# Output weights split inside the mixer's end, the last gate block after the last scores, and the first two feature tiles fetched early, in a one-core decoder layer

## The reference

```
u = x @ w_in                                # q, k, v | xr (LRU input) | yg (gate branch)
attn = sliding_window_attention(rope(q), rope(k), v, sinks)    # window 128, 8 heads, 2 kv heads
xc = causal_depthwise_conv(xr)                                 # width 4
r, i = sigmoid(xc @ w_rg + b_rg), sigmoid(xc @ w_ig + b_ig)
a = exp(-8 * r * softplus(-lam));  h_t = a_t * h_(t-1) + sqrt(1 - a_t^2) * i_t * xc_t
lru = gelu(yg) * h
mixed = concat(rmsnorm(attn) * g_attn, rmsnorm(lru) * g_lru)
h = layernorm(alpha * x + mixed @ w_out)
scores = sigmoid(h @ w_router)              # 64 experts, 8 of them chosen within 4 of 8 groups
out = layernorm(alpha * h + shared_expert(h) + sum over chosen experts of weight * expert(h))
```

## Time and profile before

| what | value |
|---|---|
| median of 3 runs | 2626.66 us |
| lowest, highest | 2623.69, 2627.61 us |
| the profiled execution | 2624.12 us |
| its span (first to last instruction) | 2622.3 us |
| busy in the span | PE 93%, PEld 75%, DVE 60%, ACT 44%, POOL 27% |
| mean granted TensorE clock | 0.965 of full speed |
| mixer | 0 to 535.8 us |
| `output_and_route` | 535.8 to about 795 us |
| `experts` | the largest part of the rest |

### The profile page before, as it was taken

The page is one execution under the profiler, slowest core; times in us unless marked ns, Lnnn a source line. Parts: engine busy times, 40 slices in busy tenths (PEclk is TensorE's granted clock), DMA queues, the critical chain, the costliest instruction groups (busy, mean ns, idle before and its releaser), DMA issues. The chain is left out here.

```text
span 2622.3 us, 48850 instructions
## 1 busy us (share of the span) xinstructions
PE 2441.9 (93%) x11925; PEld 1975.1 (75%) x11927; DVE 1569.2 (60%) x2501; ACT 1148.2 (44%) x1761; POOL 707.0 (27%) x830
## 2 busy tenths in 40 slices
PE   7899999769987989999999999999999999999990
PEld 5676767648875867888888888888888888888870
DVE  4675756647777865655565555665555555655526
ACT  4636363532212124544555444554555445554425
POOL 0000000001110003333344333343333333433435
PEclk9999999979998999999999999999999999999995
DMA  7232322174426437987888878898888878888656
GB/s 225 92 133 93 121 89 89 47 236 163 162 101 230 165 135 236 280 238 211 253 274 255 241 221 238 254 276 231 256 252 258 240 218 247 271 254 237 140 115 272
DMA packets 261956, 527.82 MB, mean 201 GB/s; under 512 B 26960, under 2 KB 172272, under 8 KB 257792
## 3 DMA queue, kind: packets, MB, share of 16 engines
q1 hardware_dynamic: 211088, 344.67, 38.3%
q0 software_dynamic: 47952, 179.70, 27.2%
q10 hardware_dynamic: 2848, 2.59, 0.4%
HBM read 388.99 MB, written 137.92 MB: 201 GB/s over the span
## 5 line engine op out<-in xcount | busy, mean ns | idle before, releaser
L2109 POOL DMA_INDIRECT acc<-y,si x164 | 298.4, 1820 | 783.6 <-DMA acc<-y,si 387.7
L2198 DVE TENSOR_TENSOR gu_lo<-raw_gu,gu_hi (+1 forms) x128 | 292.8, 2288 | 175.4 <-ACT gu_hi L2129 175.1
L2306 PE MATMUL psG<-gu_hi,xT_lo 128*128 x1320 | 348.3, 406 | 0.9 <-issue 0.8
L2295 PE MATMUL psG<-gu_hi,xT_hi 128*128 x1328 | 338.6, 397 | 3.1 <-ACT xT_hi L2125 1.6
L2295 PE MATMUL psG<-gu_lo,xT_hi 128*128 x1328 | 336.0, 395 | 0.0
L2295 PEld LDWEIGHTS psG<-gu_hi,xT_hi 128*128 128x128 f32 x1328 | 250.5, 189 | 64.1 <-issue 3.7
L2295 PEld LDWEIGHTS psG<-gu_lo,xT_hi 128*128 128x128 f32 x1328 | 249.9, 188 | 60.3
L2306 PEld LDWEIGHTS psG<-gu_hi,xT_lo 128*128 128x128 f32 x1320 | 236.6, 189 | 45.3 <-issue 1.3
L2129 ACT ACTIVATE gu_hi<-raw_gu (+1 forms) x128 | 238.1, 1908 | 47.2 <-issue 47.2
L2198 DVE TENSOR_TENSOR d_lo<-raw_d,d_hi (+1 forms) x64 | 146.7, 2293 | 150.0 <-ACT d_hi L2129 150.0
L2178 ACT ACTIVATE HT_hi<-psH 128x256 fp32r<-128x256 f32 x164 | 63.0, 384 | 381.2 <-PE psH L2313 381.2
(11 more groups left out here) (324 smaller groups left out, 3851.3 us busy)
## 6 DMA issues: line engine op xcount, KB each, us to landing
raw_gu<-in_w_gate_dram SPq DMA_DIRECT2D x64, 1024.0 KB, 6.0
raw_gu<-in_w_up_dram SPq DMA_DIRECT2D x64, 1024.0 KB, 12.2
raw_d<-in_w_down_dram SPq DMA_DIRECT2D x64, 1024.0 KB, 6.5
wring<-split_d SPq DMA_DIRECT2D x24, 1024.0 KB, 4.8
acc<-out SPq DMA_DIRECT2D x17, 512.0 KB, 3.0
split_d<-wring SPq DMA_DIRECT2D x8, 1024.0 KB, 4.9
mT<-mixed SPq DMA_DIRECT2D x16, 512.0 KB, 3.7
xt<-in_x_dram SPq DMA_DIRECT2D x16, 512.0 KB, 4.4
```

Source lines behind the costliest of these rows:

```text
L2109: nc.gpsimd.indirect_dma_start(out=acc, out_offset=bass.IndirectOffsetOnAxis(ap=si[k][:, 0:1], axis=0), in_=y[k][:], in_offset=None, compu ...
L2198: nc.vector.tensor_tensor(dst, src, hi, ALU.subtract).then_inc(dlo_s if n == 2 else gulo_s, 1)
L2295: nc.tensor.matmul(psG[slot][:], xT_hi[slot][:, c, :], right[:, bass.ds(w, 1), c, :].rearrange("p a n -> p (a n)"), start=(n == 0 and c == ...
L2306: m = nc.tensor.matmul(psG[slot][:], xT_lo[slot][:, c, :], gu_hi[:, bass.ds(w, 1), c, :].rearrange("p a n -> p (a n)"), start=False, stop= ...
```

## The change

- `wqkv`, `wring`, `xT`, `IG` and `A` are allocated before the mixer at fixed sides of the memory, and given back at once, so that `raw_gu`, `raw_d`, `wo_hi` and `wo_lo` lie on the same bytes: `wqkv_hi` and `IG` under `raw_gu`, `wring[0]` under the first slot of `raw_d`, `A` and `wqkv_lo` under `wo_hi`, `xT` under `wo_lo`. The buffer `mT` is now in that first slot of `raw_d` for all tiles.
- SP fetches three of the four pieces of `w_out` when the last k and v product is full, features 0 and 1 when gate block 2 is full, and the fourth piece when the last scan is over.
- ACT makes all eight `wo_hi` at the end of the mixer, between the last `lr_square` and `square_o(15)`. DVE makes four `wo_lo` behind `evac_o(15)`, and the other four as the first thing of the next block.
- In the last group, gate block 2 is cut in halves around the last scores, and gate block 3 comes behind them. `gelu(3)` goes behind `exps(15)`, the last `gate` behind `divide(15)`, and `evac_p(15)` ahead of the four `lru_norm`.
- `output_and_route` no longer fetches `w_out` and features 0 and 1; ACT's first copy there is `high(0)`.

```
@@ mixer, sync
+                if g + 1 == GROUPS:
+                    U["kv", TILES - 1].wait_full(sp_)
+                    for q in range(3):
+                        load_wo(q)
                 store_attention(i + 2)
                 if g + 1 < GROUPS:
                     load_split(1, g + 1)
+            U["yg", 2, GROUPS - 1].wait_full(sp_)
+            for n in range(2):
+                sp_.dma_start(mixed_view(raw_d, n), mixed[n]).then_inc(mixed_in[n], 16)
+            sp_.wait_ge(scan_s, LC * GROUPS)
+            load_wo(3)
             store_recurrent(GROUPS - 1)
             store_attention(TILES - 1)
@@ mixer, scalar
             exps(TILES - 1)
+            gelu(3, GROUPS - 1)
             for c in range(LC):
                 lr_square(c, GROUPS - 1)
+            for c in range(KC):
+                act.wait_ge(wo_in[c // 2], 32 if c < 4 else 16)
+                nc.scalar.activation(wo_hi[:, c, :], wo_view(raw_gu)[:, c, :], ACT.Copy).then_inc(wohi_s, 1)
             square_o(TILES - 1)
@@ mixer, vector
-                for c in range(LC):
+                for c in range(LC if g < GROUPS - 1 else LC - 1):
                     gate(c, g)
             divide(TILES - 1)
+            gate(LC - 1, GROUPS - 1)
+            evac_p(TILES - 1)
             for c in range(LC):
                 lru_norm(c, GROUPS - 1)
-            after_turn(TILES - 1)
+            evac_o(TILES - 1)
+            U["yg", LC - 1, GROUPS - 1].wait_full(dve)
+            for c in range(KC // 2):
+                dve.wait_ge(wohi_s, c + 1)
+                nc.vector.tensor_tensor(wo_lo[:, c, :], wo_view(raw_gu)[:, c, :], wo_hi[:, c, :],
+                                        ALU.subtract).then_inc(wolo_s, 1)
             sums(GROUPS - 1)
@@ mixer, tensor
-                tile(i + 3, lambda: project_T(6, g), last_filler)
+                if g < GROUPS - 1:
+                    tile(i + 3, lambda: project_T(6, g), last_filler)
+                else:
+                    tile(i + 3, *halves(6, g))
+                    project_T(7, g)
@@ output_and_route, sync
-            load_wo(0)
-            load_mixed(0)
-            for q in range(1, HALF):
-                load_wo(q)
             load_x(0)
-            load_mixed(1)
             load_x(1)
             sp.wait_ge(wolo_s, KC)
             prefetch(sp)
@@ output_and_route, scalar
-            for c in range(KC):
-                act.wait_ge(wo_in[c // 2], 32 if c < 4 else 16)
-                nc.scalar.activation(wo_hi[:, c, :], wo[:, c, :], ACT.Copy).then_inc(wohi_s, 1)
-                if c == 0:
-                    high(0)
+            high(0)
             scale_x(0)
@@ output_and_route, vector
+            for c in range(HALF, KC):
+                dve.wait_ge(wohi_s, c + 1)
+                nc.vector.tensor_tensor(wo_lo[:, c, :], wo[:, c, :], wo_hi[:, c, :], ALU.subtract).then_inc(wolo_s, 1)
+            low(0)
             dve.wait_ge(consts_set, 5)
             nc.vector.reciprocal(rms[:], rms[:]).then_inc(consts_set, 1)
             dve.wait_ge(consts_set, 6)
-            for c in range(KC):
-                dve.wait_ge(wohi_s, c + 1)
-                nc.vector.tensor_tensor(wo_lo[:, c, :], wo[:, c, :], wo_hi[:, c, :], ALU.subtract).then_inc(wolo_s, 1)
-                if c == 1:
-                    low(0)
             dve.wait_ge(consts_in, 16 * 6)
             low(1)
```

More of the change, by code:

```diff
@@ L91, in bcast, with wo_view, mixed_view @@
     return bass.AP(tensor=ap.tensor, offset=ap.offset, ap=pairs)
+def wo_view(raw_gu):
+    return raw_gu[:].rearrange("p s k n -> p (s k n)").rearrange("p (k n) -> p k n", n=D)
+def mixed_view(raw_d, n):
+    return raw_d[:, 0, n, :].rearrange("p (k n) -> p k n", k=KC)
 def mixer(nc, x, w_in, conv_w, conv_b, w_rg, b_rg, w_ig, b_ig, lam, sinks, g_attn, g_lru,
-          ident_h, cos_h, sin_h, mask_h, maskf_h, split_d, mixed, ssa, ssl):
+          ident_h, cos_h, sin_h, mask_h, maskf_h, split_d, mixed, ssa, ssl,
+          w_out, raw_gu, raw_d, wo_hi, wo_lo, shared, early):
+    wo_in, wohi_s, wolo_s, mixed_in = early
     spent = []
@@ L1130, in output_and_route @@
         consts_set = sem("consts2_set")
-        mixed_in = [sem(f"mixed_in{i}") for i in range(2)]
         xt_in = [sem(f"xt_in{i}") for i in range(2)]
@@ L2556, in decoder_layer, with sbu @@
         passed = ctx.enter_context(nc.semaphore("passed"))
-        spent = mixer(nc, x, w_in, conv_w, conv_b, w_rg, b_rg, w_ig, b_ig, lam, sinks, g_attn, g_lru,
-              ident_h, cos_h, sin_h, mask_h, maskf_h, split_d, mixed, ssa, ssl)
+        with ExitStack() as under:
+            def sbu(name, shape, dt, side):
+                return under.enter_context(nc.sbuf_tensor(name, shape, dt, side=side))
+            wqkv_hi = sbu("wqkv_hi", [P, KC, XR_COL], FR, "left")
+            IG = sbu("IG", [P, LC, GT], F, "left")
+            wring = [sbu(f"wring{i}", [P, 2, KC, P], FR, "left") for i in range(2)]
+            A = sbu("A", [P, LC, GT], F, "right")
+            wqkv_lo = sbu("wqkv_lo", [P, KC, XR_COL], FR, "right")
+            xT = [sbu(f"xT_{n}", [P, KC, GT], FR, "right") for n in ("hi", "lo")]
+        shared = ([wqkv_hi, wqkv_lo], wring, xT, IG, A)
         raw_gu = sb("raw_gu", [P, W_SLOTS, KC, 2 * FE])
         raw_d = sb("raw_d", [P, W_SLOTS, FE // P, D])
+        early = ([ctx.enter_context(nc.semaphore(f"wo_in{i}")) for i in range(KC // 2)],
+                 ctx.enter_context(nc.semaphore("wohi_s")), ctx.enter_context(nc.semaphore("wolo_s")),
+                 [ctx.enter_context(nc.semaphore(f"mixed_in{i}")) for i in range(2)])
+        out_weights = ExitStack()
+        wo_hi, wo_lo = (out_weights.enter_context(nc.sbuf_tensor(n, [P, KC, D], FR, side="right")) for n in ("wo_hi", "wo_lo"))
+        spent = mixer(nc, x, w_in, conv_w, conv_b, w_rg, b_rg, w_ig, b_ig, lam, sinks, g_attn, g_lru,
+              ident_h, cos_h, sin_h, mask_h, maskf_h, split_d, mixed, ssa, ssl,
+              w_out, raw_gu, raw_d, wo_hi, wo_lo, shared, early)
         loaded = [ctx.enter_context(nc.semaphore(n)) for n in ("gate_in", "up_in", "down_in")]
```

69 lines of the change are left out of this document (33 added, 36 removed).

## The result

| | before | after |
|---|---|---|
| median | 2626.02 us (4 runs, 2623.69 to 2627.61) | 2608.56 us (4 runs, 2606.57 to 2609.98) |
| profiled execution, its span | 2624.12, 2622.3 us | 2607.80, 2606.0 us |
| mean granted clock | 0.965 | 0.970 |

The ratio is 0.9934, with a 95% interval of 0.9922 to 0.9946: 17.5 us less. The forecast was 2605 (2600 to 2613), so the time lies in the range, 3.6 us above the forecast.

What follows compares the result with a forecast made beforehand. It took the mixer-to-output-stage seam, where PE is hardly at work and nothing hides a delay, as the bound. Terms -4.15 - 6.95 - 9.9 = -21.0 us took the profiled 2624.12 to 2603.1, forecast as 2605 us (range 2600 to 2613).

Steps and rivals of the forecast that it cites:

- The order's part: Last group of the mixer: reordered gate blocks start the last tile's exponentials 3.8 us earlier and `square_o` 4.1 us earlier.
- The eight copies: ACT, mixer's end: eight wo_hi copies before `square_o` take 7.7 us and cost 1.2 us there.
- The second table load: ACT, behind the last exponentials: gelu 3 needs another load of 1.29 us, with no further loss taken.
- The step that failed first: Mixer's end: `square_o` to the next block's start stays 7.04 us, so that block starts at 531.6.
- Start of the stage: Output stage: the first product starts 6.25 us into the block instead of 13.20, a gain of 6.95 us.
- late constants: Rival, output stage: DVE waits for six constants, putting tile 1 3.8 us late; 2609 us, chance 0.07.
- a late fourth fetch: Rival, mixer's end: the fourth megabyte of w_out, or the first weights, lands late; +3.5 us, 2609 us, chance 0.06.
- The first tile: Output stage, tile 0: 48 back-to-back matmuls, 9 slow and 39 fast, take 12.8 us instead of 22.72, gaining 9.9.
- a clock that stays low: Rival, output stage: low clock through the whole first tile, 20.6 us instead of 12.8; 2613 us, chance 0.06.
- The assumption under the yardstick: From tile 1's products on (571.69 us before), instructions and order are unchanged, so their shift reaches the kernel's end.
- sign of being wrong: Whole kernel, one of several listed: the end moves by other than what tile 1 moved.
- a gain that doesn't carry through: Rival, experts' stage: something keeping its own time gives the gain back; 2625 us, chance 0.04.

Runs made afterwards that it cites:

- b3_wolo_late: The changed kernel with DVE's first four wo_lo held until POOL has made the last tile's sum; 2609.19 us, ratio 0.9940 to the kernel before.
- the bare plan: The kernel before with only the change's new places in memory, old order, fetches and splitting; 2628.52 us, ratio 1.0018 to the kernel before.
- the low plan: The changed kernel with xT, A, wqkv_lo, wo_hi and wo_lo in the lower part of memory, same instructions; 2605.30 us, ratio 0.9926 to the kernel before.
- the split plan: The changed kernel with wo_hi, wqkv_lo and A low in memory, wo_lo and both parts of xT high; 2606.29 us in one run.

## Why the prediction was right, and where it wasn't

**The order's part was right up to `square_o`.** The PE was ready for PTp and waited 0.57 us for it, the mask of the second scores followed the scan at 504.49, the exponentials moved by -3.85 us for -3.8. The eight copies took 7.67 for 7.7 us and their row shows no wait for a transfer. The second table load cost what its own row says: 510.22 to 511.51, 1.29 us, starting 0.01 us behind the last instruction of the exponentials. The Trainium skill's 1.38 us of drain ("ScalarE: Activation LUTs", "What ACT_TABLE_LOAD costs") isn't in this trace; by it `square_o` would have been 1.4 us later than it was, and it was 0.4 earlier than forecast.

**The step that failed first: from `square_o` to the next block's start "535.77 - 528.73 = 7.04 us, unchanged".** It was 9.44. The forecast had put four `wo_lo` on DVE at just this time and asked only whether they were over when the sums came, not who works beside them. POOL's two additions made the way 1.45 us longer beside them, which `b3_wolo_late` shows by giving it back. The other 0.95 us is in PE's row of 16 sums, 3.55 us for 2.60. The windows view of PE over that row, before and after:

```profile
530.91:533.40 2.49, 2.49 (x17) 0.71 0.00 0
```

```profile
525.30:528.70 3.40, 3.40 (x17) 0.50 0.00 0
```

In the kernel before a short stretch at the full clock, 2.4 GHz, covered the first part of these sums (0.71 on the mean); in the changed kernel they ran wholly at the lower level, 1.2 GHz. The repeat of the kernel before had 2.72 us; the bare plan and the order alone, which have no `wo_lo` on DVE there, had 3.54 both, so it is not DVE's doing. All eleven profiles of the other kernels have 3.54 or 3.55. The 2.60 that went into the 7.04 was thus a price at a clock that the forecast had not looked up, and one that no other kernel found again. Why the fast stretch fell on the sums in both executions of the kernel before, no run tells.

**Start of the stage: -7.20 us for -6.95.** Right, and its mechanism too; the constants weren't in the way. Their last one let DVE go at 544.37, a wait of 5.81 us, and the PE needed that low part 8 us later, in tile 1's last pass. The rivals of late constants and of a late fourth fetch are out.

**The first tile: 13.43 us for 12.8.** The low clock ended within the second eight products (3.58, 2.38, then 1.87 each). I had 9 slow ones of 0.43; the first sixteen took half a us more than that, and the fast ones take 0.234 instead of 0.229, which is the plan again. In the other kernels with early weights the second eight took 1.84 to 2.92 us by where the clock rose, so this term has a spread of a us. The rival of a clock that stays low, 20.6 us, is out.

**The assumption under the yardstick failed.** "Behind it the changed kernel has the same instructions in the same order on every engine", and "so a shift at the yardstick should reach the end of the kernel". The instructions were the same, their operands were not where they had been. Fifteen tiles took 2.96 us more, and the low plan takes that back with no instruction changed. The forecast's own sign of being wrong shows it: tile 1 moved by 21.2 us, the end of the span by 16.3. The forecast noted that "only the features' buffer has another name" and never asked what else of an instruction can differ. This was the rival of a gain that doesn't carry through, in a small form and in another place: 3 us in the output stage, where it had 21 in the experts'.

**And 2.6 us came from ahead of the changed place.** They made the yardstick fit, and that was luck. Without them tile 1 would have stood at 553.1. No term of the forecast had them. They are the clock's, and the plan may have a part: the anchors differ by 1.3 us between the plans on the mean, and by a us between two executions of one kernel.

The sum of the forecast, with the terms as measured: -2.07, -7.20 and -9.29 are -18.6; +2.96 behind; -2.6 ahead and +1.9 behind the output stage. This last one is within what an execution varies: from the shared expert's first product to the end it is 1822.3 to 1825.9 us over the 13 profiles, and both ends are executions of the kernel before. That is -16.3 in the profiled pair, and -17.5 in the medians. So the time came into the range because the seam gave 18.6 of 21.0, by the mechanism forecast, less the 3 us that the new places cost. Without the 2.6 us from ahead of the place the profiled execution would have been at 2610.4, still inside.

## What to carry to other kernels

When work is moved beside other work, ask for every engine that is still on the path there whether it was alone before: POOL's 0.72 and 0.45 us held only while DVE was idle. A change of the memory plan is a change of its own, to be timed alone, even where no instruction changes: here it took back some 3 to 4 us, and another plan with the same overlaps gave them back in both pairs, each within overlapping intervals. Measure a gain from an anchor just ahead of the changed place; a yardstick counted from the kernel's start took in 2.6 us that the order and the early weights had not made. And look at the granted clock of every short row whose time goes into a sum: the sums of squares were 2.60 us or 3.55 by it.

## What the runs showed of the hardware

- Matmuls of 128 x 512 at full clock followed each other at 227.9 ns (mixer) and 229.3 (output stage) or at 232.4 and 233.9, by the memory plan alone, the same within 0.1 ns in every execution of these two plans; the split plan had 232.7 and 230.1. The experts' stage had 232.3 on the mean in all, and in one execution of the changed kernel 234.2 for its first third: so not all of such a difference is the plan.
- The mixer with the shorter distance had more low clock (0.98 granted from 45 to 489 us, against 0.99), and on the mean of 5 and 8 profiles reached its last group 1.3 us later.
- Two DVE subtractions and two POOL additions side by side cost POOL 1.47 us and DVE 0.78.
